# A projection stage with its triangular solution, gate columns and value columns in another order

## Chip, cores and metric

The kernel runs on one core of one Trainium2 chip. The metric is the device time in microseconds (us) of one execution; three executions of the kernel before are given. The engines are PE (TensorE, matmuls), PEld (its weight loads), DVE (VectorE), ACT (ScalarE), POOL (GpSimd) and SP (SyncE, which here only issues DMAs). Each runs its own list of instructions in order and waits on semaphores for the others.

## What is computed

A decoder trunk of two layers on x of 1024 tokens by 1024 features, float32. Only layer 0 is touched by the change:

```python
hn = rmsnorm(x, norm_w[0])
proj = hn @ w_in                                   # 1024 x IN0
gq, gk, gv, g_low, rw, gate = split(proj)          # q, k, values, low-rank gate input, RWKV part, gate
log_decay = log_sigmoid(g_low @ gk_up + gk_bias) / 16
o_a = gla_chunked(gq, gk, gv, log_decay)           # cumulated decay inside chunks of 64 tokens
...                                                # r, k, v, decay, a from rw with a token shift
o_b = rwkv7_scan(r, decay, k, v, -kk, kk * a)      # done in chunks of 64 tokens
o = concat(o_a, o_b) * silu(gate)
h = x + o @ w_out
```

The chunked form of the RWKV scan needs, for each chunk and head, the inverse of a unit triangular 64x64 matrix. In the kernel this is "the solution" (`solve`). There are 128 such matrices (16 chunks x 8 heads), one on each partition.

## The kernel before

All of layer 0's input projection is one stage, `project0`. It computes 30 weight tiles of 128 output features, called tile 0 to tile 29 by their turn. A tile is 48 matmuls of 128x512: eight k blocks, two halves of 512 tokens, and three products, since each float32 factor is split into a rounded high part and a low rest (`WH`, `WL` for the weights, `HNH`, `HNL` for the activations). `W0_ORDER` says which weights come in which turn:

- tile 0, and tiles 1 to 12: the shifted inputs and r, k, v for four pairs of heads. DVE and ACT work them up (`mix`, `keep_raw`).
- tiles 13 to 20: the gate. ACT applies SiLU (`keep_gate`) into `gate_row` and stores it to `gate_dram`.
- tile 21: the low-rank gate input (16 rows). Four small matmuls (L495) turn it into the decay's argument.
- tiles 22 to 25: q and k of the gated linear attention, kept in `QK` (`keep_qk`).
- tiles 26 to 29: its values, kept in `GV`.

What each engine does for a tile: SP loads its weights (`WA`, `WBK` or `WRAW`), POOL makes the high part (L1371) and the low part (L1375) once the tile two before is done (`split_parts`), PE waits for both parts and for `tile_kept` of the tile two before (its PSUM banks), ACT copies the result out of PSUM.

The solution runs on DVE. ACT stores the pairs' masked products to `bonds_dram` (`store_bonds`), loads them back with one matrix per partition into `X` (L569), and DVE does 62 steps of one multiplication and one addition (L666, L669). `X` lies in the four rows of `GV`, its product `TMP` in a row of `QK`. So tile 25 (the last row of `QK`) is kept only when the solution is over (`act.wait_ge(solved, ...)`). Then ACT stores `X` to `solved_dram`, waits for that, and only then uses `GV` for the decay of the linear attention: bias, absolute value, exponential, logarithm, a masked cumulated sum over 1024 tokens (L720), exponentials. DVE multiplies q and k with these (L728). Only then are tiles 26 to 29 kept in `GV`.

A block of code ends for all engines together (a barrier). The next one, `chunks0`, walks through the 1024 tokens in eight steps of two chunks. It loads the inverses (`TT0`, `TTB`) and the gate (`SG`) back from memory.

Of the kernel before, what the change touches and what calls it, by code (L numbers as in the profile page):

```python
# [22 lines left out]
F = mybir.dt.float32  # L23
# [7 lines left out]
P = 128  # L31
T = 1024
# [30 lines left out]
W0_GATE = 13  # L63
W0_GLOW = 21
W0_GLA = 22
W0_TILES = 30
W0_ORDER = list(range(13)) + list(range(22, 30)) + list(range(13, 22))
# [4 lines left out]
def trunk(nc, x, w0t, wup, gkup, wout0, w1t, wv1, bv1, wout1, par, bout1, fnorm, ident_d, istack_d, bdones_d,  # L72
          maska_d, scan_d, maskd_d, maskb_d, cos_d, sin_d, band_d, out):
    root = ExitStack()
    with root:
# [132 lines left out]
        with layer0:  # L208
# [3 lines left out]
            QK = VQ[:, PAIRS:, :].rearrange("p (a q) t -> p a q t", a=2)  # L212
# [3 lines left out]
            TT0 = [RAW[:, 1 - n // 2, n % 2 * HB:(n % 2 + 1) * HB].rearrange("p (q m) -> p q m", m=C) for n in range(4)]  # L216
            bonds_dram = nc.dram_tensor("bonds_dram", (TT, 2, PAIRS, 2, C, C), F, kind="Internal").ap()
            solved_dram = nc.dram_tensor("solved_dram", (TT, 2, PAIRS, 2, C, C), F, kind="Internal").ap()
            solved_out = sem("solved_out")
            G = sb("G", [P, PAIRS, NC], ctx=layer0)  # L220
# [4 lines left out]
            gate_out = sem("gate_out")  # L225
            half1 = ExitStack()
            with half1:
# [9 lines left out]
                WRAW = RAW[:, 0, 0:T].rearrange("p (k c) -> p k c", k=KT)  # L237
# [14 lines left out]
                with nc.Block() as block:  # L252
                    @block.sync
                    def _(sp):
# [7 lines left out]

                project0(nc, sem, PS, HNH, HNL, WA, WBK, WRAW, WH, WL, parts, wup_sb, xw, gkup, gate_row,
                         gate_dram, gate_out, RAW, scanm, scan_d, AR, BK, VT, QK, GV, bdones, G, GG, small, w0t, col, const2_in,
                         w_in, maska, TT0, bonds_dram, solved_dram, solved_out)
# [4 lines left out]
            with loop:  # L270
                chunks0(nc, sb, sem, loop, PS, AR, BK, VT, QK, GV, G, GG, small, ident, istack, maska, bdones, TT0,
                        solved_dram, solved_out, SG, col("gla_norm"), bk_tiles, wout0, wo_in, gate_dram, gate_out)
# [71 lines left out]

def project0(nc, sem, PS, HNH, HNL, WA, WBK, WRAW, WH, WL, parts, wup_sb, xw, gkup, gate_row, gate_dram,
             gate_out, RAW, scanm, scan_d, AR, BK, VT, QK, GV, bdones, G, GG, small, w0t, col, const_in, w_in, maska,
             TT0, bonds_dram, solved_dram, solved_out):

# [5 lines left out]
    mixd, kmix, kk, sa = (QK[:, i // 2, i % 2, :] for i in range(4))  # L354
    nrm, cum, e2, sw = (GV[:, i, :] for i in range(4))
    e1a, sq, scan_again = sw, nrm, gate_row
    gk_sb = kmix[0:16, 0:256]
    PAIRED = 3 * PAIRS + 1
    X = GV[:, :, :].rearrange("p a t -> p (a t)").rearrange("p (j i) -> p j i", i=C)
    ST, TMP = kmix, sa  # L360

    def arrival(n):
        return WA[:] if n % 2 == 0 or n == PAIRED else WBK if n < PAIRED else WRAW
# [32 lines left out]
    with nc.Block() as block:  # L396
        @block.sync
        def _(sp):
            sp.dma_start(scanm, scan_d).then_inc(scan_in, 16)
            for n in range(2, W0_TILES):  # L400
# [12 lines left out]
            sp.wait_ge(g_rel, GP)  # L413
# [4 lines left out]
            sp.wait_ge(tt0_in, 64)  # L418

        @block.gpsimd  # L420
        def _(pool):
            for n in range(2, W0_TILES):
                pool.wait_ge(w_in[n % 2], 16 * (n // 2) + 16)
                pool.wait_ge(tile_done, n - 1)
                split_parts(pool, arrival(n), WH[:, n % 2], WL[:, n % 2], 2 * n, parts)

        @block.tensor
        def _(pe):
# [57 lines left out]
            tile(W0_GATE, W0_GATE % 2)  # L486
            bonds(PAIRS - 1)
            for n in range(W0_GATE + 1, W0_GLA + 1):
                tile(n, n % 2)
# [3 lines left out]
            for j in range(GP):  # L493
                for h in range(2):
                    last = pe.matmul(PS[4 + 2 * j + h][:], gk_sb[:, j * P:(j + 1) * P], mixd[0:16, h * HB:(h + 1) * HB],  # L495
                                     start=True, stop=True)
                last.then_inc(gz_done, 1)

            for n in range(W0_GLA + 1, W0_TILES):
                tile(n, n % 2)  # L500
# [1432 lines left out]
```

## Time and profile before

| | |
|---|---|
| median of 3 executions | 1244.69 us (1243.75 to 1245.27) |
| the profiled execution's own time | 1252.05 us |
| its span | 1249.8 us |
| PE busy / PEld busy | 1124.4 us (90%) / 899.1 us (72%) |
| DVE / ACT / POOL busy | 662.6 / 332.7 / 294.0 us |
| mean granted TensorE clock | 0.95 of full speed |

All times inside the kernel below are microseconds from the start of the profiled span. `project0` fills the stretch from about 30 us to 446 us, `chunks0` follows until about 625 us. The profile gives PE's busy share in 40 slices of 31 us; it is 90% or more for nearly all of `project0`, but 6, 4 and 5 tenths in the slices that hold 344 to 437 us. Idle time before an instruction is put down to the instruction that released it.

### The profile page before, as it was taken

Reading aid. Unit: us, or ns where it says so; the run is one execution under the profiler, and the core shown is the slowest. Engines: PE = TensorE matmul, PEld = TensorE weight load, DVE = VectorE, ACT = ScalarE, POOL = GpSimd, SP = SyncE. Lnnn points to the kernel's source line nnn. Section 1 sums busy time; section 2 is a strip of 40 time slices with the busy share of each in tenths; the row PEclk is TensorE's granted clock in tenths of the full one; section 3 lists DMA queues with packets and bytes.
Section 4 is the critical chain, followed back from the end, with each engine's and each line's share of the span. In section 5 each row is a group of like instructions: output and inputs, shape, how many; then the busy total and the mean of one; then the engine's idle time right before and its main releaser. Section 6 shows DMA issues by size and latency. Waiting matters only on the chain. (4 is left out here: it accounts for less than half of the span.)

```text
span 1249.8 us, 20321 instructions
## 1 busy us (share of the span) xinstructions
PE 1124.4 (90%) x8408; PEld 899.1 (72%) x8408; DVE 662.6 (53%) x1031; ACT 332.7 (27%) x749; POOL 294.0 (24%) x190
## 2 busy tenths in 40 slices
PE   3999999999964578898889997999999899998997
PEld 3777777888753468787734446888888788887886
DVE  5288898499995315344434115255510258987233
ACT  6333423101103314233241003011110224554121
POOL 2222322334331011010000004133322534440500
PEclk9999999999987799999989998999999959999999
DMA  5211211632111060200204201111111010131011
GB/s 193 68 51 35 53 49 41 214 101 84 34 51 67 18 186 3 70 3 3 70 1 184 102 34 63 51 42 42 50 50 34 35 51 18 35 133 34 17 51 68
DMA packets 37577, 77.77 MB, mean 62 GB/s; under 512 B 19184, under 2 KB 19712, under 8 KB 37120
## 3 DMA queue, kind: packets, MB, share of 16 engines
q1 hardware_dynamic: 27616, 66.23, 15.9%
q10 hardware_dynamic: 9888, 10.49, 2.6%
q8 instruction: 56, 0.92, 0.3%
q14 instruction: 17, 0.14, 0.0%
HBM read 59.93 MB, written 16.78 MB: 61 GB/s over the span
## 5 line engine op out<-in xcount | busy, mean ns | idle before, releaser
L1383 PE MATMUL ps<-HNH,WH 128*128 128x512 f32 x896 | 356.2, 398 | 51.1 <-ACT GV L508 25.8
L1383 PE MATMUL ps<-HNH,WL 128*128 128x512 f32 x896 | 352.4, 393 | 0.0
L1383 PE MATMUL ps<-HNL,WH 128*128 128x512 f32 x896 | 352.0, 393 | 0.0
L1383 PEld LDWEIGHTS ps<-HNH,WH 128*128 128x128 f32 x896 | 170.4, 190 | 89.9 <-issue 54.4
L1383 PEld LDWEIGHTS ps<-HNH,WL 128*128 128x128 f32 x896 | 170.8, 191 | 36.3 <-issue 1.2
L1383 PEld LDWEIGHTS ps<-HNL,WH 128*128 128x128 f32 x896 | 170.6, 190 | 36.4
L1282 PE MATMUL ps<-BK,SG 128*128 128x512 f32 x256 | 112.8, 601 | 1.4 <-PEq L787 1.4
L1282 PEld LDWEIGHTS ps<-BK,SG 128*128 128x128 f32 x256 | 49.3, 193 | 63.7 <-issue 63.7
L1744 ACT ACTIVATE GV<-GV,nm 128x256 f32<-128x256 f32 x128 | 64.3, 504 | 78.6 <-DVE nm L1765 78.3
L666 DVE TENSOR_TENSOR VQ<-GV 128x62 f32<-128x62 f32 (+30 forms) x62 | 71.4, 1152 | 20.2 <-DMA GV<-bonds_dram 18.1
L1704 PE MATMUL ps<-V,GV 128*128 (+1 forms) x512 | 73.2, 292 | 0.8 <-DVE GV L1778 0.7
L1704 PEld LDWEIGHTS ps<-V,GV 128*128 128x128 f32 x512 | 70.9, 214 | 2.5 <-issue 1.3
L1765 DVE CUSTOM_DVE_ANT_0 GV<-ps,GV,nsink 128x256 f32<-128x256 f32 x128 | 56.8, 481 | 29.1 <-PE ps L1383 21.6
L669 DVE TENSOR_TENSOR GV<-GV,VQ 128x62 f32<-128x62 f32 (+30 forms) x62 | 68.9, 1111 | 2.1
L1371 POOL CAST WH<-WA 128x1024 fp32r<-128x1024 f32 x16 | 20.8, 1297 | 147.2 <-PE ps L1383 130.8
L508 ACT ACTIVATE RAW<-ps 128x512 f32<-128x512 f32 x42 | 22.9, 597 | 115.6 <-PE ps L1383 105.8
L1371 POOL CAST WH<-GV 128x1024 fp32r<-128x1024 f32 x18 | 18.7, 1041 | 145.3 <-PE ps L1383 138.8
L1693 PE MATMUL ps<-ident,GV 128*128 128x128 f32 x256 | 47.4, 314 | 0.5 <-ACT GV L1744 0.5
L1778 DVE COPY GV<-ps 128x512 f32<-128x512 f32 x64 | 44.0, 688 | 1.0 <-PE ps L1693 0.9
L1361 DVE TENSOR_TENSOR H<-ps,AR 128x512 f32<-128x512 f32 x16 | 10.3, 686 | 64.6 <-PE ps L1282 61.0
L1816 DVE TENSOR_SCALAR nsink<-par 128x16 f32<-128x16 f32 x1 | 1.0, 1039 | 81.1 <-PEq L1515 81.1
L1375 POOL TENSOR_TENSOR WL<-GV,WH 128x1024 fp32r<-128x1024 f32 x18 | 43.2, 2400 | 3.0 <-POOL WH L1371 2.9
(246 smaller groups left out, 1728.9 us busy)
## 6 DMA issues: line engine op xcount, KB each, us to landing
GV<-in_w1t SPq DMA_DIRECT2D x18, 512.0 KB, 3.6
AR<-in_x SPq DMA_DIRECT2D x16, 512.0 KB, 7.1
WA<-in_w0t SPq DMA_DIRECT2D x16, 512.0 KB, 3.6
RAW<-in_w0t SPq DMA_DIRECT2D x8, 512.0 KB, 3.7
gate_dram<-RAW ACTq DMA_DIRECT2D x8, 512.0 KB, 2.6
SG<-gate_dram SPq DMA_DIRECT2D x1, 4096.0 KB, 15.4
BK<-in_wout SPq DMA_DIRECT2D x4, 1024.0 KB, 6.8
h_dram<-H SPq DMA_DIRECT2D x8, 512.0 KB, 2.6
```

Source lines behind the costliest of these rows:

```text
L508: ins = act.activation(dst[:, h * HB:(h + 1) * HB], tile_bank[n % 2][h][:], func, **kw)
L666: dve.tensor_tensor(tmp, X[:, j:j + 1, j + 1:C].to_broadcast([P, j, n]), X[:, 0:j, j:j + 1].to_broadcast([P, j, n]), ALU.mult).then_inc(so ...
L669: dve.tensor_tensor(X[:, 0:j, j + 1:C], X[:, 0:j, j + 1:C], tmp, ALU.add).then_inc(solved, 1)
L1282: last = pe.matmul(PS[2 * (t % 4) + h][:], SG[:, k, t * P:(t + 1) * P], W[:, k, h * HB:(h + 1) * HB], start=(k == 0), stop=(k == KT - 1))
L1371: eng.tensor_copy(high, raw).then_inc(parts, 1)
L1375: eng.tensor_tensor(low, raw, high.bitcast(F), ALU.subtract).then_inc(parts, 1)
L1383: last = pe.matmul(out, a, b, start=(k == 0 and i == 0), stop=(k == n - 1 and i == 2))
L1693: last = pe.transpose(PS[4 + j % 2][:, (2 * a + b) * P:(2 * a + b + 1) * P], PR[:, j % 2, a, b * P:(b + 1) * P], ident[:])
L1704: last = pe.matmul(PS[6 + j // HT][:, (j % HT) * P + a * C:(j % HT) * P + (a + 1) * C], PT[:, j % 2, a, b * P:(b + 1) * P], V1[:, ds(n + b ...
L1744: ins = act.activation(PR[:, j % 2, a, :], SC[:, j % 2, a, :], ACT.Exp, scale=-1.0, bias=nm[:, h:h + 1], accum_out=rs[:, h:h + 1])
L1765: ins = dve.tensor_tensor_reduce(SC[:, j % 2, a, :], PS[2 * (j % 2) + a][:, 0:2 * P], band[:, 0 if first else 1, :], -1.0, nsink[:, h:h + ...
L1778: dve.tensor_copy(PT[:, j % 2].rearrange("p a k -> p (a k)"), PS[4 + j % 2][:]).then_inc(s["pt_kept"], 1)
```

## The change

Four parts lie in `project0`, the fifth in `chunks0`.

1. **Order of the tiles.** Tile 13 is now the low-rank gate input, tiles 14 and 15 the first two gate tiles, 16 to 19 the values, 20 to 23 q and k, 24 to 29 the other six gate tiles.
2. **Places.** `X` now lies in the upper half of `VQ` (`XS`), the product `TMP` in the first row of `RAW` (`solve_row`). Every gate, value, q and k tile is kept in the one `gate_row`; values go out to a new `value_dram`. The decay's rows and, after them, q and k lie in `GV`. The third arrival place for weights, `WRAW`, is gone: from tile 13 on every tile's weights arrive in `WA`.
3. **Work on the engines.** The decay's work on DVE stands inside the solution: `gate_sizes` before step 10, `gate_sums` before step 26. The cumulated sum is 16 scans of 64 tokens instead of one of 1024. From tile 16 on ACT makes the high part of the weights (`high_part(n + 2)`, ahead of keeping tile n). POOL makes the low part only, and multiplies q and k with their factors. SP stores the finished `X`.
4. **Waits.** The solution's end holds up no tile. The load of tile 14's weights now stands behind SP's wait for `pair_done` of the fourth pair. The block's end waits for the inverses of the first two steps, all gate stores and all value stores.
5. **`chunks0`.** The values are loaded back in two halves (`VG`), ahead of the gate. The zeroing of `S` and `GS` moves from DVE to POOL. PE waits for `consts` only ahead of the matmuls with `cen`.

```diff
-W0_ORDER = list(range(13)) + list(range(22, 30)) + list(range(13, 22))
+W0_ORDER = list(range(14)) + [22, 23] + list(range(18, 22)) + list(range(14, 18)) + list(range(24, 30))
...
     def arrival(n):
-        return WA[:] if n % 2 == 0 or n == PAIRED else WBK if n < PAIRED else WRAW
+        return WA[:] if n % 2 == 0 or n >= PAIRED else WBK
...
             for n in range(2, W0_TILES):
-                sp.wait_ge(parts, 2 * n if n in (PAIRED, PAIRED + 1) else 2 * n - 2)
-                if n == PAIRED + 2:
-                    sp.wait_ge(mixed, PAIRED)
-                if n == PAIRED + 5:
-                    sp.wait_ge(ab_out, 64 * PAIRS)
+                sp.wait_ge(parts, 2 * n if n >= PAIRED else 2 * n - 2)
+                if n == W0_GLOW + 1:
+                    sp.wait_ge(pair_done, PAIRS)
                     sp.dma_start(gk_sb, gkup).then_inc(gk_in, 16)
                 sp.dma_start(arrival(n), w0t[W0_ORDER[n]]).then_inc(w_in[n % 2], 16)
-            sp.wait_ge(gate_out, 16 * KT)
-            sp.dma_start(scan_again, scan_d).then_inc(gk_in, 16)
+            sp.wait_ge(solved, 2 * (C - 2))
+            sp.dma_start(solved_dram.rearrange("n e p h j i -> (n e p h) j i"), X).then_inc(solved_out, 16)
             sp.wait_ge(solved_out, 16)
-            sp.wait_ge(g_rel, GP)
             for n in range(2):
                 for e in range(2):
                     sp.dma_start(TT0[n][e * C:(e + 1) * C], solved_dram[n, e].rearrange("p h j m -> j (p h) m")
                                  ).then_inc(tt0_in, 16)
             sp.wait_ge(tt0_in, 64)
+            sp.wait_ge(gate_out, 16 * KT)
+            sp.wait_ge(value_out, 16 * 4)
...
                 pool.wait_ge(tile_done, n - 1)
-                split_parts(pool, arrival(n), WH[:, n % 2], WL[:, n % 2], 2 * n, parts)
+                if n < CAST:
+                    split_parts(pool, arrival(n), WH[:, n % 2], WL[:, n % 2], 2 * n, parts)
+                else:
+                    pool.wait_ge(parts, 2 * n + 1)
+                    pool.tensor_tensor(WL[:, n % 2], arrival(n), WH[:, n % 2].bitcast(F), ALU.subtract).then_inc(parts, 1)
+                if W0_QK <= n - 2 < W0_QK + 4:
+                    j = n - 2 - W0_QK
+                    pool.wait_ge(tile_kept, n - 1)
+                    pool.wait_ge(g_exp, GP)
+                    pool.tensor_tensor(GV[:, j, :], GV[:, j, :], gate_row, ALU.mult).then_inc(g_scaled, 1)
...
+            def high_part(n):
+                if n < W0_TILES:
+                    act.wait_ge(w_in[n % 2], 16 * (n // 2) + 16)
+                    act.wait_ge(tile_done, n - 1)
+                    act.activation(WH[:, n % 2], arrival(n), ACT.Copy).then_inc(parts, 1)
...
-            act.wait_ge(solved, 2 * (C - 2))
-            keep_qk(3)
-            act.dma_start(solved_dram.rearrange("n e p h j i -> (n e p h) j i"), X).then_inc(solved_out, 16)
-            act.wait_ge(solved_out, 16)
...
+            def gate_sums():
+                for j in range(GP):
+                    z, l = (nrm, cum)[j], (e2, sw)[j]
+                    dve.wait_ge(gz_step, GP + j + 1)
+                    link(dve.scalar_tensor_tensor(out=z, in0=z, scalar=0.0, in1=l, op0=ALU.min, op1=ALU.subtract))
+                    for c in range(NC):
+                        ins = dve.tensor_tensor_scan(l[:, c * C:(c + 1) * C], chunk_mask[:], z[:, c * C:(c + 1) * C], 0.0,
+                                                     ALU.mult, ALU.add)
+                    link(ins)
+                    relative(l, z, GG[:, j, :])
+                    dve.tensor_copy(mid, mid).then_inc(g_rel, 1)
...
                 for j in range(1, C - 1):
+                    if j == EARLY:
+                        gate_sizes()
+                    if j == LATE:
+                        gate_sums()
```

ACT's row in the program before, from the store of the last pair's products on (names: `GV` holds `X` and then the decay, `VQ` holds q and k, `RAW` the gate row):

```order
L521 DMA bonds_dram<-VQ 64x8x64 x4
L569 DMA GV<-bonds_dram 128x4096
...
L562 DMA gate_dram<-RAW 128x1024
L574 ACTIVATE VQ<-ps 16x512 x2
L578 ACTIVATE small<-small 128x1
L508 ACTIVATE VQ<-ps 128x512 x8
L589 DMA solved_dram<-GV 128x4096
L594 ACTIVATE GV<-ps,par 128x512 x4
```

ACT's row after, of the same place and of the first value tile behind it (`VQ` holds `X`, `WH` is a high part):

```order
L536 DMA bonds_dram<-VQ 64x8x64 x4
L616 DMA VQ<-bonds_dram 128x4096
L577 ACTIVATE WH<-WA 128x1024
L523 ACT_TABLE_LOAD
L523 ACTIVATE RAW<-ps 128x512 x2
L597 DMA gate_dram<-RAW 128x1024
L622 ACTIVATE GV<-ps,par 128x512 x4
...
L577 ACTIVATE WH<-WA 128x1024
L523 ACTIVATE RAW<-ps 128x512 x2
L603 DMA value_dram<-RAW 128x1024
```

The store of the solution has left ACT's row, the decay's first step stands ahead of the second gate tile, and a high part stands ahead of each kept tile.

DVE's row after, around step 26 of the solution (`RAW` is the product, `VQ` is `X`, `GV` the decay's rows; the scans are printed as L704). Before, steps 25 and 26 stood side by side:

```order
L726 TENSOR_TENSOR VQ<-VQ,RAW 128x25x38
L702 SCALAR_TENSOR_TENSOR GV<-GV 128x1024
L704 SCALAR_TENSOR_TENSOR GV<-chunk_mask,GV 128x64 x16
...
L708 COPY small<-small 128x16
L702 SCALAR_TENSOR_TENSOR GV<-GV 128x1024
L704 SCALAR_TENSOR_TENSOR GV<-chunk_mask,GV 128x64 x16
...
L708 COPY small<-small 128x16
L723 TENSOR_TENSOR RAW<-VQ 128x962
```

The decay's sums now delay the solution's second half.

SP's row after, at the end of `project0`:

```order
L413 DMA GV<-in_gkup 16x256
L414 DMA WA<-in_w0t 128x1024 x16
L417 DMA solved_dram<-VQ 128x4096
L421 DMA RAW<-solved_dram 64x8x64 x4
L403 UNCONDITIONAL_BRANCH
```

All 16 weight loads from tile 14 on stand behind the load of `gk_sb`, and the solution's store and reload come last.

## Rows read from the trace of the kernel before

**Rows 1.** Who PE waited for, 200 to 450 us: total, times, longest
```profile
PE ps L1383 <- ACT GV L508: 25.8, 1, 25.8
PE ps L1383 <- ACT VQ L508: 18.7, 1, 18.7
```

**Rows 2.** Timeline of ACT: start, duration, line, operation, idle before and its releaser
```profile
227.22 1.09 ACT L508 ACTIVATE RAW<-ps 128x512 f32<-128x512 f32 x2 [8.04 <-PE ps L1383]
...
380.66 0.60 ACT L508 ACTIVATE VQ<-ps 128x512 f32<-128x512 f32 x1 [38.15 <-DVE GV L669]
...
419.86 2.07 ACT L508 ACTIVATE GV<-ps 128x512 f32<-128x512 f32 x4 [4.77 <-DVE VQ L728]
433.77 1.09 ACT L508 ACTIVATE GV<-ps 128x512 f32<-128x512 f32 x2 [11.85 <-PE ps L1383]
444.65 1.09 ACT L508 ACTIVATE GV<-ps 128x512 f32<-128x512 f32 x2 [9.79 <-PE ps L1383]
```

**Rows 3.** Timeline of POOL: splits of tiles 14, 22 and 29
```profile
204.18 1.04 POOL L1371 CAST WH<-WA 128x1024 fp32r<-128x1024 f32 x1 [10.16 <-PE ps L1383]
205.31 2.39 POOL L1375 TENSOR_TENSOR WL<-WA,WH 128x1024 fp32r<-128x1024 f32 x1
...
305.55 3.22 POOL L1375 TENSOR_TENSOR WL<-RAW,WH 128x1024 fp32r<-128x1024 f32 x1
...
395.43 1.04 POOL L1371 CAST WH<-RAW 128x1024 fp32r<-128x1024 f32 x1 [28.22 <-PE ps L1383]
```

**Rows 4.** A stretch of PE: length, PE busy, granted clock, DMA share, GB/s
```profile
384.00:386.00 2.00, 2.00 (x6) 0.50 1.13 483
```

**Rows 5.** Timeline of DVE: solution's start, steps at 304 us, decay
```profile
236.12 0.18 DVE L666 TENSOR_TENSOR VQ<-GV 128x62 f32<-128x62 f32 x1 [18.07 <-DMA GV<-bonds_dram]
...
304.61 1.91 DVE L669 TENSOR_TENSOR GV<-GV,VQ 128x990 f32<-128x990 f32 x1
306.55 3.27 DVE L666 TENSOR_TENSOR VQ<-GV 128x992 f32<-128x992 f32 x1
309.85 1.19 DVE L669 TENSOR_TENSOR GV<-GV,VQ 128x992 f32<-128x992 f32 x1
...
408.55 2.29 DVE L720 TENSOR_TENSOR_SCAN GV<-RAW,GV 128x1024 f32<-128x1024 f32 x1
...
411.29 0.18 DVE L643 TENSOR_TENSOR GG<-GG,GV 128x15 f32<-128x15 f32 x1
411.51 1.23 DVE L644 TENSOR_TENSOR GV<-GV,small 128x1024 f32<-128x1024 f32 x1
```

**Rows 6.** Timelines of DVE and ACT around the last pair, 212 to 226 us
```profile
212.93 1.22 DVE L706 TENSOR_TENSOR BK<-VQ,GV 128x1024 f32<-128x1024 f32 x1
216.77 1.29 DVE L652 TENSOR_TENSOR VQ<-ps,maska 128x512 f32<-128x512 f32 x2
219.61 3.61 ACTq L521 DMA_DIRECT2D bonds_dram<-VQ  x4
225.24 0.34 ACTq L569 DMA_DIRECT2D GV<-bonds_dram  x1
```

**Rows 7.** DMAs by line (L408 weights, L589 solution out, L416 inverses in), and page part 6
```profile
DMA to landing us min/median/max: 3.5/3.6/7.2
...
DMA to landing us min/median/max: 6.3/6.3/6.3
...
DMA to landing us min/median/max: 3.0/3.2/3.8
...
gate_dram<-RAW ACTq DMA_DIRECT2D x8, 512.0 KB, 2.6
```

**Rows 8.** The same rounding cast on ACT in layer 1, from the critical chain
```profile
1149.93 1.07 ACT WH L1432
```

**Rows 9.** Timelines of SP and PE where `chunks0` starts
```profile
446.00 1.25 SPq L792 DMA_DIRECT2D RAW<-solved_dram  x2
...
448.04 1.07 PE L840 MATMUL ps<-ident,AR 128*128 128x128 f32 x4 [3.43 <-DVE cen L1226]
```

More of the change, by code:

```diff
@@ L270, in trunk @@
             with loop:
-                chunks0(nc, sb, sem, loop, PS, AR, BK, VT, QK, GV, G, GG, small, ident, istack, maska, bdones, TT0,
+                chunks0(nc, sb, sem, loop, PS, AR, BK, VT, QK, XS, value_dram, value_out, G, GG, small, ident, istack, maska, bdones, TT0,
                         solved_dram, solved_out, SG, col("gla_norm"), bk_tiles, wout0, wo_in, gate_dram, gate_out)
@@ L485, in _ @@
                     low_rank(p + 1)
-            tile(W0_GATE, W0_GATE % 2)
+            tile(W0_GLOW, W0_GLOW % 2)
             bonds(PAIRS - 1)
-            for n in range(W0_GATE + 1, W0_GLA + 1):
-                tile(n, n % 2)
+            tile(W0_GLOW + 1, (W0_GLOW + 1) % 2)
             pe.wait_ge(glow_kept, 1)
@@ new lines, in keep_gate, with keep_value @@
+            def keep_gate(n):
+                staged(n)
+                keep(n, gate_row, ACT.Silu)
+                act.wait_ge(tile_kept, n + 1)
+                act.dma_start(gate_dram[W0_GATES.index(n)], gate_row).then_inc(gate_out, 16)
+            def keep_value(n):
+                staged(n)
+                keep(n, gate_row, ACT.Copy)
+                act.wait_ge(tile_kept, n + 1)
+                act.dma_start(value_dram[n - W0_VALUE], gate_row).then_inc(value_out, 16)
+            act.wait_ge(pair_done, PAIRS)
@@ L608, in _ @@
                 act.activation(z, z, ACT.Exp, scale=1.0 / NORMALIZER).then_inc(g_exp, 1)
-            act.wait_ge(g_scaled, 4)
             for j in range(4):
-                keep(W0_GLA + 4 + j, GV[:, j, :], ACT.Copy)
+                staged(W0_QK + j)
+                keep(W0_QK + j, gate_row, ACT.Copy, scale=GLA_SCALE if j < 2 else 1.0)
+            for n in W0_GATES[2:]:
+                keep_gate(n)
         @block.vector
@@ L655, in keep_bonds, with gate_sizes @@
                 ins.then_inc(ab_kept, 1)
+            def gate_sizes():
+                for j in range(GP):
+                    z, l = (nrm, cum)[j], (e2, sw)[j]
+                    dve.wait_ge(gz_kept, j + 1)
+                    dve.scalar_tensor_tensor(out=l, in0=z, scalar=-1.0, in1=z, op0=ALU.mult, op1=ALU.max).then_inc(gz_abs, 1)
+            def gate_sums():
+                for j in range(GP):
+                    z, l = (nrm, cum)[j], (e2, sw)[j]
+                    dve.wait_ge(gz_step, GP + j + 1)
[6 more added lines that the diff above has]
+                    dve.tensor_copy(mid, mid).then_inc(g_rel, 1)
             def solve():
@@ L765, in chunks0 @@
     s = {n: sem("c_" + n) for n in names.split()}
-    tt_in = [sem(f"c_tt_in{n}") for n in range(NP)]
+    tt_in = {n: sem(f"c_tt_in{n}") for n in range(2, NP)}
+    vg_in = [sem(f"c_vg_in{h}") for h in range(2)]
     def after(eng, name, n):
@@ L795, in _ @@
             sp.wait_ge(solved_out, 16)
-            inverses(2)
+            sp.wait_ge(value_out, 16 * 4)
+            for h in range(2):
+                cols = slice(h * HB, (h + 1) * HB)
+                sp.dma_start(VG[:, :, cols], value_dram[:, :, cols].rearrange("k p t -> p k t")).then_inc(vg_in[h], 16)
+                inverses(2 + h)
             sp.wait_ge(gate_out, 16 * KT)
             sp.dma_start(SG[:], gate_dram.rearrange("k p t -> p k t")).then_inc(s["gate_in"], 16)
-            for n in range(3, NP):
+            for n in range(4, NP):
                 inverses(n)
@@ L841, in turns_av @@
                 last.then_inc(s["r1a"], 1)
+                if n == 0:
+                    pe.wait_ge(s["consts"], 1)
                 for p in range(PAIRS):
@@ L939, in step @@
                 after(pe, "s_kept", 2 * n + e)
+                if n == 0 and e == 0:
+                    pe.wait_ge(s["zeros"], 1)
                 if e == 0:
```

127 lines of the change are left out of this document (63 added, 64 removed).

## The prediction, made before the changed kernel ran

> **What bounds the kernel now.** I read PE's waits first, since PE is busy 90% of the span and every stage hangs on it. Two stalls inside `project0` stand out: 18.7 us before tile 27 and 25.8 us before tile 28 [rows 1]. ACT's timeline gives their cause [rows 2]: the keeping of tile 25 waits 38.15 us for the solution's last addition (L669) and comes at 380.66, and the keeping of tile 26 waits for L728 until 419.86. After each stall PE runs at half clock for a while: 0.50 granted, the 1.2 GHz level, at 384 to 386 us after 18.7 us of idleness [rows 4]. An undisturbed tile takes 444.65 − 433.77 = 10.88 us [rows 2]. Tile 27 took 395.43 − 381.8 = 13.6 [rows 2, 3], 2.7 too long. Tile 28 took 433.77 − (395.43 + 25.8) = 12.5, 1.7 too long. So the solution and the decay cost PE 18.7 + 25.8 + 2.7 + 1.7 = 48.9 us here. `chunks0` starts on SP at 446.00 and on PE at 448.04 [rows 9].
>
> After the change two chains run side by side, and the later one sets the block's end: the stream of tiles on PE, and the solution on DVE with its way through memory. I work out both.
>
> **The stream of tiles.** It ends at 444.65 now. Without the stalls it would end at 444.65 − 48.9 = 395.8. A new stall comes in at tile 14, because SP's load of its weights now stands behind `pair_done` of pair 4, which DVE gives at 212.93 + 1.22 = 214.15 [rows 6]. Two issues take about 0.4, landing takes 3.6 [rows 7] and the split 1.04 + 0.08 + 2.39 = 3.5 [rows 3]. That makes 221.7. Before, split 14 was over at 207.7 [rows 3] and tile 14 ended at 227.22 [rows 2], so it started at 216.3. PE is then idle for some 5.5 us. It then runs at half clock for a while: I charge 1.8, near the 1.7 of tile 28, where the bounds are 0 and 2.7. Behind it in SP's queue stand the loads of all later tiles, each one split behind. They have time: tile 14 itself now ends at about 234.5. The small matmuls L495 move from after tile 22 to after tile 14 at the same price. The stream ends at 395.8 + 5.5 + 1.8 = 403.1. Keeping tile 29 takes 1.1 and its store 0.4 + 2.6 [rows 2, 7]: the stream's part of the block is over at 407.2.
>
> High parts on ACT cost PE nothing: the cast takes 1.07 on ACT [rows 8] against 1.04 on POOL, and per tile ACT has 1.07 + 1.09 us of work in 10.88. If ACT sits in a wait when a tile ends, its cast comes late, and POOL's low part with it. The cover is 10.88 − 1.07 − 3.2 = 6.6 us per tile. The tightest place is tile 20: ACT must first have the decay's exponentials, which need `gate_sums`. By the chain below these end at about 302, the exponentials 3 us later, and tile 20 is done at about 305. That costs nothing as long as the sums are over by 308.
>
> **The solution.** ACT now issues the last pair's stores at 216.77 + 1.29 = 218.1 instead of 219.61, since no gate tile stands ahead of them. So X is loaded at 225.24 − 1.5 = 223.7 and the first step comes at 236.12 − 1.5 = 234.6 [rows 5, 6]. The steps took 380.6 − 236.1 = 144.5 us. What changes in them:
> - POOL's casts go. The step at 304.61 took 1.91 beside a cast and the next 3.27 beside a subtraction, against 1.19 undisturbed [rows 5]: 0.72 for a cast, 2.08 for a subtraction. Twelve splits fell into the solution, so −12 × 0.72 = −8.6.
> - The solution lasts longer and starts earlier, so it meets two more subtractions: +2 × 2.08 = +4.2.
> - Four multiplications of q and k on POOL, each a two-input operation like the subtraction: +4 × 2.08 = +8.3. Bounds: 0 if they fall beside nothing, 4 × 3.22 = 12.9 [rows 3] if each blocks DVE for its whole span.
> - `gate_sizes`: 2 × 1.23 = +2.5 [rows 5]. ACT adds the bias within some 8 us of tile 14's end, by 243; by the sizes of the first nine steps the tenth starts 11 us after 234.6. So no wait, with 3 us to spare.
> - `gate_sums`, twice: 1.23 + 1.23 for the two long operations, four short ones of about 0.2, and sixteen scans of 64. A scan of 1024 takes 2.29 and an operation of 15 elements 0.18 [rows 5], so one of 64 is 0.18 + 64/1024 × 2.1 = 0.31 by itself. Without a wait between them their fixed parts overlap partly: bounds 0.14 and 0.31, taken 0.21. That is 16 × 0.21 + 2.46 + 0.8 = 6.6, twice = +13.2. Bounds 10.9 and 16.5.
>
> The sum is 144.5 − 8.6 + 4.2 + 8.3 + 2.5 + 13.2 = 164.1, and the solution ends at 234.6 + 164.1 = 398.7. The store lands 6.3 later [rows 7]. Four loads follow, 0.65 apart and 3.2 to land [rows 7]: 5.2. With 0.3 for the barrier the next block starts at 398.7 + 6.3 + 5.2 + 0.3 = 410.5. That is 3 us behind the stream, so the solution still sets the end, now through memory and no longer through ACT's queue.
>
> The Trainium skill speaks against the short scans: VectorE: DVE Perf Modes, in the section on the TRN2 errata, says that SBUF operands cost a fixed time per instruction, many small tiles pay it each, and operands should have 512 elements or more. By its (N + 151)/0.96 ns rule for a float32 operation, the 30 extra scans cost 30 × 0.157 = 4.7 us, an estimate from that page; with it the sum would be some 2.7 us longer. The trace's nearest row is the 0.18 of 15 elements, which agrees in size and says nothing on overlap.
>
> **`chunks0`.** PE started 2.04 after the block because it waited for `cen` behind two memsets. Now the transposes start at once, at 410.6, and `cen` is ready under them. The loads of the values and the gate are needed only one step later, behind other work. PE will have been idle for 7 us, before it was 3.43 us [rows 9]. A colder start can cost up to tile 28's 1.7; I charge 0.5, since the clock may already have fallen in the shorter pause.
>
> **The sum.** PE's start in `chunks0` moves from 448.04 to 410.6 + 0.5 = 411.1: 36.9 us less. Later stages are the same instructions in the same order. Against the profiled execution that is 1252.05 − 36.9 = 1215.1. That execution is 7.4 above the median, so in the median 1244.69 − 36.9 = **1207.8 us**.
>
> **The rivals.**
> *The tiles end last.* If POOL's multiplications cost DVE nothing and the scans are cheap, the solution's end moves up by 10, but the stream's end at 407.2 + 0.3 stays: 3 us less, 1204.8. For it: the two chains are 3 us apart on 160. Against it: all twelve splits disturb DVE alike.
> *The solution is longer.* Whole-span blocking by POOL (+4.6), scans without overlap (+3.3) make 1215.7. The Trainium skill's SBUF — State Buffer, on who interferes with whom, has DVE and GpSimd hold a shared port exclusively for a whole instruction and the other block fully; an estimate by it is that +4.6. The trace shows 2.08 of 3.22 per subtraction, less than that rule read at its worst.
> *A stall inside the stream.* `gate_sums` wait for late logarithms or ACT's cast for late exponentials, at tiles 20 to 22. The first 3 us are covered by the solution. Beyond them each us counts: with 8 us of stall, 1212.8.
> *Slower than before: one arrival place.* From tile 13 on the load of tile n + 1 waits for the low part of tile n. The loop is landing + ACT's cast + POOL's subtraction, 3.6 + 1.1 + 3.2 = 7.9 of 10.88 us. It decides from a landing of 6.6 on; one load did take 7.2, beside X's load [rows 7]. With 10 us each the 14 tiles would take 3.4 × 14 = 48 longer and give back all: 1244.69 + 8 = 1253. Nothing moves much data during those tiles except stores of 512 KB, so I hold it unlikely.
> *The change doesn't do what it says.* Tile 27 could still wait for something of DVE's. Its keep now waits only for the gate's store, so this is part of the second last case.
>
> **How the numbers follow.** Forecast as worked out, 1206 to 1210: 0.45. Tiles end last: 0.20, 1203 to 1206. Longer solution: 0.18, 1210 to 1217. Stall inside the stream: 0.14, 1208 to 1216. One arrival place: 0.03. The range 1203 to 1215 leaves out about 0.2. A measurement of this kernel tells apart about 0.2% (2.5 us). All cases but the last lie far beyond it: faster 0.96, same 0.01, slower 0.03.
>
> **What would show it.** In the changed kernel's profile: no PE wait over 10 us in `project0`, one of about 5.5 before tile 14, and tiles 10.88 apart from tile 16 on. Steps of the solution beside POOL show one lengthened operation per tile, not two. The scans stand about 0.2 apart. The last L726 comes at about 399, and the first inverses land at about 410, after the last gate store. PE's first wait in the next block is for nothing of DVE's constants. It is wrong if the last store of a gate tile comes later than the inverses, or if PE waits for `parts` from tile 16 on.

## The result and the profile after

The changed kernel takes 1206.42 us (median of four executions; 1244.79 before), a ratio of 0.9668 with a 95% interval of 0.9615 to 0.9722. An execution that ran as a whole at a lower granted clock, here one of 1242.50 us, is left out of this and every later ratio, while the medians hold all. Forecast were 1207.8 us, 1203 to 1215. The profiled execution took 1206.31 us with a span of 1204.5.

PE's waits in `project0` and at the start of `chunks0` in the changed kernel (who waited for whom: total, times, longest). Against [rows 1] both long stalls are gone. The new one before tile 14 is there; the second row is the pause at the block's end:

```profile
PE ps L1435 <- POOL WL L1427: 5.9, 1, 5.9
PE ps L887 <- PEq L403: 4.3, 1, 4.3
```

ACT's timeline of the changed kernel: the last two gate tiles and the store of the last (start, duration, line, operation, idle before). The tiles stand 10.88 apart up to the end, against [rows 2]:

```profile
391.79 1.09 ACT L523 ACTIVATE RAW<-ps 128x512 f32<-128x512 f32 x2 [8.84 <-PE ps L1435]
...
402.67 1.09 ACT L523 ACTIVATE RAW<-ps 128x512 f32<-128x512 f32 x2 [9.79 <-PE ps L1435]
403.79 0.33 ACTq L597 DMA_DIRECT2D gate_dram<-RAW  x1
```

POOL's timeline of the changed kernel, the split of tile 14 (compare the first two of [rows 3]):

```profile
217.57 1.04 POOL L1423 CAST WH<-WA 128x1024 fp32r<-128x1024 f32 x1 [24.30 <-DMA WA<-in_w0t]
218.68 2.34 POOL L1427 TENSOR_TENSOR WL<-WA,WH 128x1024 fp32r<-128x1024 f32 x1
```

DVE's timeline of the changed kernel: the solution's first product, the second row of scans, two products beside POOL's subtraction and multiplication, and the last addition (compare [rows 5]):

```profile
230.09 0.18 DVE L723 TENSOR_TENSOR RAW<-VQ 128x62 f32<-128x62 f32 x1 [12.72 <-DMA VQ<-bonds_dram]
...
290.84 3.03 DVE L704 TENSOR_TENSOR_SCAN GV<-chunk_mask,GV 128x64 f32<-128x64 f32 x16
...
306.41 3.26 DVE L726 TENSOR_TENSOR VQ<-VQ,RAW 128x986 f32<-128x986 f32 x1
309.70 2.87 DVE L723 TENSOR_TENSOR RAW<-VQ 128x990 f32<-128x990 f32 x1
312.60 1.19 DVE L726 TENSOR_TENSOR VQ<-VQ,RAW 128x990 f32<-128x990 f32 x1
...
391.03 0.28 DVE L726 TENSOR_TENSOR VQ<-VQ,RAW 128x62 f32<-128x62 f32 x1
```

The timelines of SP and PE of the changed kernel at the end of the block (compare [rows 9]):

```profile
391.34 0.33 SPq L417 DMA_DIRECT2D solved_dram<-VQ  x1
397.81 2.71 SPq L421 DMA_DIRECT2D RAW<-solved_dram  x4
406.94 0.39 SPq L840 DMA_DIRECT2D VQ<-value_dram  x1
...
406.91 1.09 PE L887 MATMUL ps<-ident,AR 128*128 128x128 f32 x4 [4.34 <-PEq L403]
```

And what SP waited for last in `project0`:

```profile
SPq L425 <- DMA gate_dram<-RAW: 5.9, 1, 5.9
```

PE starts `chunks0` at 406.91 instead of 448.04, 41.1 us earlier. The last wait of the block is for the store of the last gate tile (L425), not for the inverses. Four inverse loads leave SP from 397.81 on over 2.71 us, and the gate store is issued at 403.79. Their times to landing (the loads of L421, then all gate stores of L597, of which the last took 2.6):

```profile
DMA to landing us min/median/max: 2.9/3.0/3.1
...
DMA to landing us min/median/max: 2.6/2.6/6.0
```

So the last inverse is there at about 402.9 and the gate store at 406.4. The solution, forecast to end the block, had 3.5 us of slack in this profile, and the stream of tiles ended it.

The spans differ by 45.3 us and the medians by 38.4. The stages behind `project0` explain this. The next views show them for the kernel before and for the changed one: `chunks0` with the output mix up to the load of x; from there to attention; attention up to the reload of h. The columns are the stretch, its length, PE's busy time with its instructions, the granted clock, and the share and GB/s of DMA.

Kernel before:

```profile
446.00:671.76 225.76, 192.10 (x3689) 0.96 0.15 46
671.76:991.13 319.37, 310.68 (x1305) 0.99 0.18 64
991.13:1113.12 121.99, 119.74 (x912) 0.83 0.12 35
```

Changed kernel:

```profile
406.90:635.53 228.63, 196.72 (x3689) 0.94 0.18 55
635.53:953.18 317.65, 308.89 (x1305) 0.99 0.19 64
953.18:1068.40 115.22, 113.29 (x909) 0.88 0.12 37
```

The block's start moves by 39.1 us. Then `chunks0` takes 2.9 longer at a granted clock of 0.94 instead of 0.96, the middle 1.7 less, and attention 6.8 less at 0.88 instead of 0.83. The code of the last two is the same. The profiled execution of before lay 7.4 us above its median, and its attention ran long at half clock; the last section returns to this. A fairer pair is the profile of before and the second one of the changed kernel (the first experiment), whose attention took 122.0 and 121.7 us: there the spans, 1249.8 and 1210.0, differ by 39.8.

### The profile page after: what moved, and what is told of

Same layout as the page of the kernel before. It is cut to its first block and busy times, and to the rows that moved or that the text cites. A ratio compares the mean times of both kernels' runs of the same rounds, so it can differ in the third digit from the quotient of the medians.

```text
span 1204.5 us, 20383 instructions
## 1 busy us (share of the span) xinstructions
PE 1117.0 (93%) x8408; PEld 893.1 (74%) x8408; DVE 652.9 (54%) x1055; ACT 344.0 (29%) x762; POOL 286.5 (24%) x182
## 5 line engine op out<-in xcount | busy, mean ns | idle before, releaser
L723 DVE TENSOR_TENSOR RAW<-VQ 128x62 f32<-128x62 f32 (+30 forms) x62 | 66.2, 1068 | 14.8 <-DMA VQ<-bonds_dram 12.7
L726 DVE TENSOR_TENSOR VQ<-VQ,RAW 128x62 f32<-128x62 f32 (+30 forms) x62 | 71.9, 1160 | 2.1
L1756 PE MATMUL ps<-V,GV 128*128 (+1 forms) x512 | 70.3, 284 | 0.8 <-DVE GV L1830 0.7
L1756 PEld LDWEIGHTS ps<-V,GV 128*128 128x128 f32 x512 | 67.7, 206 | 2.4 <-issue 1.2
L436 POOL TENSOR_TENSOR WL<-WA,WH 128x1024 fp32r<-128x1024 f32 x14 | 40.1, 2866 | 104.7 <-ACT WH L577 104.7
L1423 POOL CAST WH<-GV 128x1024 fp32r<-128x1024 f32 x18 | 18.7, 1041 | 143.6 <-PE ps L1435 137.3
L523 ACT ACTIVATE RAW<-ps 128x512 f32<-128x512 f32 x58 | 31.3, 592 | 67.2 <-PE ps L1435 67.2
L577 ACT ACTIVATE WH<-WA 128x1024 fp32r<-128x1024 f32 x14 | 14.9, 1062 | 120.4 <-PE ps L1435 120.4
L1413 DVE TENSOR_TENSOR H<-ps,AR 128x512 f32<-128x512 f32 x16 | 10.3, 686 | 64.6 <-PE ps L1334 60.9
```

Of the source, the lines that this page charges most:

```text
L436: pool.tensor_tensor(WL[:, n % 2], arrival(n), WH[:, n % 2].bitcast(F), ALU.subtract).then_inc(parts, 1)
L523: ins = act.activation(dst[:, h * HB:(h + 1) * HB], tile_bank[n % 2][h][:], func, **kw)
L723: dve.tensor_tensor(tmp, X[:, j:j + 1, j + 1:C].to_broadcast([P, j, n]), X[:, 0:j, j:j + 1].to_broadcast([P, j, n]), ALU.mult).then_inc(so ...
L726: dve.tensor_tensor(X[:, 0:j, j + 1:C], X[:, 0:j, j + 1:C], tmp, ALU.add).then_inc(solved, 1)
L1423: eng.tensor_copy(high, raw).then_inc(parts, 1)
L1756: last = pe.matmul(PS[6 + j // HT][:, (j % HT) * P + a * C:(j % HT) * P + (a + 1) * C], PT[:, j % 2, a, b * P:(b + 1) * P], V1[:, ds(n + b ...
```

## The experiments

In what follows, PE's start of `chunks0` is counted from the keeping of tile 12 (ACT's line L508 or L523, a few lines off in some edited kernels, at 201.7 to 204.1 us), since the program's first stages shift by some 2 us from one execution to the next. In the changed kernel's three profiles it is 203.6, 202.5 and 203.8. "View A" is that the stream of tiles with its last store ends the block, "view B" the prediction's, that the solution does.

### The changed kernel again

> The changed kernel once more, unaltered, as the measure for the runs beside it. Inside project0 and at the start of chunks0 its times should repeat those of its first profile to 0.3 us: last tile kept from 402.7, the solution's last addition over at 391.3, PE's first matmul of chunks0 at 406.9. What should differ from execution to execution is the length of the half-clock stretch at the start of layer 1's attention (27 us in the first profile, 40 us in that of the kernel before). If that stretch alone carries the spread of 1197 to 1206 us, then the difference of this run's span from 1204.5 is half the difference of the stretches.

Median 1208.29 us, ratio to before 0.9657 (0.9597 to 0.9718). The profiled execution took 1211.82. PE started `chunks0` at 404.17, 2.7 us earlier than first seen, more than the 0.3 expected: 1.6 of it lie ahead of tile 12's keeping and 1.1 in the stream. Behind the small matmuls that follow tile 14 (L510) the first profile has PE at half clock from 238.3 to 241.7 (0.51 granted), the second does not (1.00). The solution's store landed after 7.4 us and not 6.5, so the last inverse was there at 402.5, only 1.1 us ahead of the last gate store (403.7). Attention took 121.7 us against 115.2 in the first profile and the stage ahead of it 1.8 more; less the earlier start this makes about the 5.5 by which the span is longer. So most of the spread inside one kernel is the clock of the later stages. The expected half of the difference in half-clock time would be 6.8 for attention (41.0 against 27.3 us); it was 6.5.

### Tile 14's weights first

```diff
-                if n == W0_GLOW + 1:
-                    sp.wait_ge(pair_done, PAIRS)
-                    sp.dma_start(gk_sb, gkup).then_inc(gk_in, 16)
                 sp.dma_start(arrival(n), w0t[W0_ORDER[n]]).then_inc(w_in[n % 2], 16)
+                if n == W0_GLOW + 1:
+                    sp.wait_ge(pair_done, PAIRS)
+                    sp.dma_start(gk_sb, gkup).then_inc(gk_in, 16)
```

> Tile 14's weights are loaded ahead of the wait for the fourth pair, only the small load for the decay stays behind it. Both views: the 5.9 us stall before tile 14 and about 2 us of half clock behind it go, the last tile is kept from 394.7 instead of 402.7. View A (in the changed kernel the stream of tiles with its last gate store ends the block, the inverses are there 3.5 us earlier): PE starts chunks0 3.6 us earlier, at 403.3, set now by the inverses. View B (the prediction's: the solution ends the block): PE starts at 406.9 as before, gain 0.

The stall is gone and the last tile is kept from 395.33. From the keeping of tile 12 that is 193.3 us instead of 199.3: 6.0 us and not 8, since part of the half clock behind the stall came back elsewhere. SP's waits at the block's end:

```profile
SPq L417 <- DVE VQ L726: 21.7, 1, 21.7
SPq L421 <- DMA solved_dram<-VQ: 6.0, 1, 6.0
SPq L425 <- DMA gate_dram<-RAW: 1.7, 1, 1.7
SPq L403 <- DMA RAW<-solved_dram: 1.3, 1, 1.3
```

PE's start comes 200.1 from tile 12's keeping, 3.4 us earlier than in the changed kernel's first profile and 2.3 earlier than in its second. View A gave 3.6, view B 0. Now the inverses end the block by 1.3 us, and only about half of what the stream gained is seen. Median 1197.51 us, 0.9602 (0.9541 to 0.9663). That is 10.8 under the changed kernel's 1208.29, three times what the start gained; in the profiled execution attention took only 105.5 us, so the medians do not measure this edit.

### High parts on POOL again

```diff
-    CAST = W0_GLOW + 3
+    CAST = W0_TILES
...
     (high_part issues nothing)
```

> The high parts of tiles 16 to 29 are made by POOL again, as in the kernel before; all else as in the changed kernel. Each of the 13 splits that fall into the solution should lengthen it by 0.72 us, 9.4 in all: last addition over at 400.7, inverses at 412.3. Tiles stay 10.88 apart. View A: PE starts chunks0 at 412.6, 5.7 us later (9.4 less the 3.5 of slack). View B: 9.4 us later. A third view, that ACT's casts do not matter because DVE isn't slowed by a cast: no change.

DVE's timeline beside one split shows both lengthened operations again, and the third is the one beside a multiplication:

```profile
306.12 1.89 DVE L726 TENSOR_TENSOR VQ<-VQ,RAW 128x972 f32<-128x972 f32 x1
308.04 3.25 DVE L723 TENSOR_TENSOR RAW<-VQ 128x980 f32<-128x980 f32 x1
311.32 2.86 DVE L726 TENSOR_TENSOR VQ<-VQ,RAW 128x980 f32<-128x980 f32 x1
```

The solution takes 171.5 us (230.2 to 401.7) against 161.2: 10.3 longer, expected 9.4. The expectation counted 13 casts inside the solution and there are 14: 14 × 0.72 = 10.1. PE starts `chunks0` at 413.59, 210.1 from tile 12's keeping, 6.6 later. View A gave 5.7, or 6.8 with the 10.3, and view B 9.4, or 10.3. PE's waits in the stream are unchanged. So ACT's casts shorten the solution, and 3.7 us of that were not needed. Median 1215.69 us, 0.9729 (0.9666 to 0.9792).

### The solution made longer

```diff
+                    if 50 <= j < 57:
+                        dve.wait_ge(solved, 2 * (j - 1))
+                        link(dve.tensor_tensor(TMP, TMP, XS[:, 0, :], ALU.mult))
```

> Seven additional multiplications of 1024 elements stand in the solution (steps 50 to 56), 7 x 1.26 = 8.8 us of DVE, and nothing else changes. View A (3.5 us of slack): PE starts chunks0 5.3 us later, at 412.2. View B (no slack): 8.8 us later, at 415.7.

The solution takes 8.9 us more. PE's first matmul of `chunks0`:

```profile
412.55 1.09 PE L890 MATMUL ps<-ident,AR 128*128 128x128 f32 x4 [10.76 <-PEq L403]
```

That is 208.8 from tile 12's keeping, 5.2 later than in the first profile, 6.3 later than in the second. View A gave 5.3 and view B 8.8. The slack was thus 3.7 us measured from the first profile and 2.6 from the second, whose stream was 1.1 us faster. Median 1217.85 us, 0.9724 (0.9665 to 0.9783).

### No wait for stores at the block's end

```diff
             sp.wait_ge(tt0_in, 64)
-            sp.wait_ge(gate_out, 16 * KT)
-            sp.wait_ge(value_out, 16 * 4)
...
                 sp.dma_start(VG[:, :, cols], ...).then_inc(vg_in[h], 16)
-                inverses(2 + h)
             sp.wait_ge(gate_out, 16 * KT)
+            for h in range(2):
+                inverses(2 + h)
```

> The end of project0 no longer waits for the gate and value stores; chunks0 waits for the gate stores before it writes the second pair of inverses over the gate row. If the last gate store ends the block in the changed kernel (view A), PE starts chunks0 once tile 29 is kept, 1.4 us after its last matmul instead of 4.2 us: 2.8 us earlier, at 200.8 us from the keeping of tile 12 instead of 203.6. If the inverses end it (view B), nothing moves. The second pair of inverses comes about 2 us later and costs nothing.

PE starts at 405.19, 201.3 from tile 12's keeping. That is 2.3 us earlier than in the changed kernel's first profile, but the edit's share is less: the stream was as fast here as in the second profile (no half clock behind the small matmuls), and against that the start is 1.2 earlier. PE's pause at the block's end says the same: 3.22 us against 4.34 and 4.37. So the stores did end the block, as in view A, but only 1.1 of view A's 2.8 came. The solution's store took 7.4 us to land here and not 6.5 (399.61 is the first inverse's issue), so the inverses ended the block, right behind. Its times (1195 to 1225, median 1217.4) say nothing of the edit: in the profiled execution attention alone took 133.9 us, at a granted clock of 0.75.

### The decay's sums at step 34

```diff
-    EARLY, LATE = 10, 26
+    EARLY, LATE = 10, 34
```

> The decay's sums stand before step 34 of the solution instead of step 26, all else as in the changed kernel. Eight steps of 2.4 us and one or two of POOL's subtractions come ahead of them, 22 us, so the sums end at 319 and ACT's exponentials at 323 instead of 302. ACT then casts tile 22's high part from 323 and POOL's low part is done at 327, while PE wants tile 22 at 315.6. Expected: one PE wait of 11 us before tile 22 with 2 us of half clock behind it, last tile kept 13 us later, PE's start of chunks0 13 us later. The prediction's rival of a stall inside the stream has this price per us; its cover of 3 us at tile 20 means that step 26 to 28 costs nothing. If the cover is larger than thought, the wait is shorter by as much.

PE's waits:

```profile
PE ps L1435 <- POOL WL L436: 11.2, 1, 11.2
PE ps L1435 <- POOL WL L1427: 5.8, 1, 5.8
```

One wait of 11.2 us for tile 22's low part, as expected. PE starts `chunks0` at 420.30, 216.6 from tile 12's keeping: 13.0 later, and 13 was expected. The rival of a stall inside the stream has its price right, and it did not happen because the sums came in time. Median 1212.52 us, though its attention ran nearly all at full clock (105.5 us).

### One wait put back

```diff
             def keep_gate(n):
                 staged(n)
+                if n == 25:
+                    act.wait_ge(solved, 2 * (C - 2))
```

> The changed kernel with one wait put back: ACT keeps tile 25 only when the solution is over, as in the kernel before (there the fourth tile of q and k, here a gate tile, whose storage has nothing to do with the solution). Expected: tile 26 is done at about 370, tile 27 waits for the keeping of tile 25 until about 392.5, so one PE wait of 22 us with 2 to 3 us of half clock behind it; last tile kept 25 us later and PE's start of chunks0 25 us later than in the changed kernel, at 228.5 from the keeping of tile 12. If the gain came from elsewhere than this wait and the decay behind it, the start moves by clearly less.

```profile
PE ps L1437 <- ACT RAW L523: 18.4, 1, 18.4
PE ps L1437 <- POOL WL L1429: 5.8, 1, 5.8
```

The stall is 18.4 us, where the kernel before had 18.7 [rows 1]. PE starts `chunks0` at 427.99, 224.3 from tile 12's keeping, 20.8 us later. Expected were 22 and 25. The solution ended at 387.6 here, 3.7 earlier than in the changed kernel, since a stopped stream makes no weight parts on POOL either: 12 subtractions fell into it and not 14, at 2.08 us each. Median 1227.07 us, 0.9847 (0.9805 to 0.989), against 1207.54 for the changed kernel on the same chip: 19.5 us. So this one wait, with no other part undone, costs half of the gain. The other half is put down to the decay's work, which stood behind the solution and made the second stall of 25.8 us [rows 1], and which stays inside it here; no run puts that back.

### `chunks0` with the constants of before

```diff
-            pool.memset(S[:], 0.0).then_inc(s["zeros"], 1)
-            pool.memset(GS[:], 0.0).then_inc(s["zeros"], 1)
...
+            dve.memset(S[:], 0.0).then_inc(s["zeros"], 1)
+            dve.memset(GS[:], 0.0).then_inc(s["zeros"], 1)
...
+            pe.wait_ge(s["consts"], 1)
             turns_av(0)
```

> In chunks0 S and GS are zeroed by DVE ahead of cen and PE waits for it at the start, as in the kernel before; project0 as in the changed kernel. Expected: PE's first matmul of chunks0 comes 2.0 us after the block's start instead of 0, and the first matmul with the inverses (line of solve) 11.0 instead of 9.3 us after it. If PE's start was bound by the clock or by ACT anyway, the second number stays within 0.5 of 9.3.

PE's first matmuls and the first with an inverse:

```profile
408.75 1.12 PE L885 MATMUL ps<-ident,AR 128*128 128x128 f32 x4 [6.33 <-DVE cen L1276]
...
416.95 1.96 PE L937 MATMUL ps<-AX,RAW 64*64 64x128 f32 x32 [0.70 <-ACT AX L1114]
```

PE's first matmul is 2.0 late, but the first with an inverse comes 10.2 us after the block's start, where 11.0 was expected and the changed kernel's first profile has 9.3: 0.9 of the 2.0 reaches it. The stretch from the block's start to the load of x took 225.7 us against 228.0 to 228.8 in the changed kernel. That looked as if the edit cost more than it gains; the last experiment tests it. Median of two executions 1210.46 us, 0.971 (0.9653 to 0.9767).

### Both ends overlapped

```diff
                 (tile 14's weights first, as above)
...
-            sp.wait_ge(solved_out, 16)
-            for n in range(2):
-                for e in range(2):
-                    sp.dma_start(TT0[n][e * C:(e + 1) * C], ...).then_inc(tt0_in, 16)
-            sp.wait_ge(tt0_in, 64)
-            sp.wait_ge(gate_out, 16 * KT)
-            sp.wait_ge(value_out, 16 * 4)
...
             sp.wait_ge(solved_out, 16)
+            inverses(0)
+            inverses(1)
             sp.wait_ge(value_out, 16 * 4)
...           (inverses of steps 2 and 3 behind gate_out, as above)
-                if n >= 2:
-                    pe.wait_ge(tt_in[n], 32)
+                pe.wait_ge(tt_in[n], 32 if n >= 2 else 64)
```

> Three edits on the changed kernel: tile 14's weights first (as in e1), no wait for stores at the block's end (as in e4), and the solution's way through memory reaches into chunks0: its store is waited for there and PE waits for the first inverses ahead of the first use, 9.3 us into the block. Expected: last tile kept from 395, PE starts chunks0 at 396.7, 10.2 us earlier than in the changed kernel and 5.5 earlier than in e1; inverses of steps 0 and 1 land at 403, before their use at 406, so no new wait. Median of all 10 us under the changed kernel's. Rival: PE then waits at the first use for the inverses (5 us or more), since their loads compete with those of values and gate; then the gain is about 5.

> The changed kernel again, for a comparison with the two below on the same chip. PE's start of chunks0 202.4 to 203.6 us after the keeping of tile 12; from the block's start to the load of x behind chunks0 228.0 to 228.6 us, as in its first two profiles.

> The overlap version again, beside the changed kernel: PE's start of chunks0 at 192.3 from the keeping of tile 12, 10 to 11 us ahead of the changed kernel's; median of the undisturbed runs 7 to 11 us lower. If chunks0 eats the gain (it took 229.7 us in this version's first profile, 1 to 2 more than in the changed kernel), the difference is nearer to 7.

The changed kernel's third profile has 203.8 and 228.8 us, each 0.2 above what was expected. In the overlap version's first profile PE starts `chunks0` at 395.44, 192.1 from tile 12's keeping: 11.5 us ahead of the changed kernel's first, where 10.2 were expected. At the first use of the inverses it then waits a little:

```profile
PE ps L936 <- DMA RAW<-solved_dram: 1.4, 1, 1.4
```

The median was 1199.70 us, 0.9618 (0.9573 to 0.9664). In the second profile it starts 195.2 from that point, 2.9 later than expected, and does not wait there for the inverses at all. The stream alone was 3.2 us longer, with 6.8 us at half clock from 227.3 on that the first profile does not have. Beside the changed kernel on one chip the medians are 1196.25 and 1207.54 us, with ratios to before of 0.9598 (0.9568 to 0.9629) and 0.9696 (0.9665 to 0.9726): 11 us less. Its start gained 8.5 in this profile and 11.5 in the other. The ratio of the version with tile 14's weights first alone, 0.9602, cannot be told from either, since attention's chance lengths lie on all of them. Spans of profiles with the same attention can be compared. With 115.3 us of it, the overlap version's 1194.4 stands 10.1 and 10.7 below the changed kernel's 1204.5 and 1205.1. With 105.5 us, its 1182.7 stands 7.2 below the 1189.9 of tile 14's weights alone. So this is the fastest version by its profiles; the medians do not show it.

### The same with the constants of before

> The overlap version with the constants of chunks0 as in the kernel before. With the constants put back, the stretch from chunks0's start to the load of x took 225.7 us against 228.0 to 228.6 with the changed constants. View C (the constants' edit starts PE 1.9 us earlier but costs the block more than that, through a colder clock in its first steps): the stretch is 2 to 3 us shorter than in the overlap version and the whole kernel 1 to 3 us faster. View D (the 225.7 was chance, PE's clock in that stretch varies by this much): the stretch is as long or up to 2 us longer than in the overlap version, and the kernel is no faster.

Median 1198.93 us, 0.9632 (0.9599 to 0.9665), against 1196.25 with the changed constants. The stretch from the block's start to the load of x took 229.8 us, as long as in the overlap version's first profile (230.0), while that version's second took 224.3. View D holds: one and the same kernel shows 230.0 and 224.3, with 27 and 17 us at half clock. The 225.7 above also had 17, against 24 to 30 in the changed kernel. So it was the clock's chance, and no loss by the edit is shown. Nor is a gain; the 2 us of an earlier start are below what the spread lets one see.

## Why the prediction came out, and what was off

**The stalls' price.** 48.9 us for the two stalls and the half clock behind them were right: with them taken off and the new stall put on, the last tile was to be kept from 403.1; it was 402.67. Putting back the one wait gives a stall of 18.4.

**The new stall.** Forecast 5.5 us, found 5.9 (5.7 to 5.9 in all profiles that have it). Tile 14 ran from 221.07 to ACT's cast at 234.01, 2.1 over the undisturbed 10.88, and 1.8 was charged.

**The solution: the step that failed.** It was to end at 398.7 and ended at 391.3, so it did not end the block. By the prediction's own sign (wrong if the last gate store comes later than the inverses) this step failed. It began 4.5 us too late in the sum and was taken 2.9 too long (164.1 against 161.2):
- its start, 230.1 instead of 234.6. X's load was taken with the 10.7 us of before; it took 7.8. The stores ahead of it were issued in 2.66 us instead of 3.61 [rows 6], and the early stages were 0.7 us faster;
- POOL's multiplications: 2.87 against 1.19 beside each, 1.7 and not 2.08, 1.6 us in all;
- the sums: 6.3 each and not 6.6, without the subtraction that fell into each. Sixteen scans took 3.03 us, 0.19 each, against 2.29 for the one long scan;
- the sizes and the casts that went: 0.3 each.

The number of POOL's subtractions inside was right: 14, of which 12 lengthened a step by 2.1 and two a sum. Why X's load was shorter stays open. In the nine profiles where the code is the same up to it, it took 7.6 to 8.0 us in eight and 10.0 in one (the decay's sums at step 34); in the versions with tile 14's weights first it took 8.9 to 10.3. The solution's store took 6.3 to 7.4 in most profiles, 8.4 and 9.2 in one each. With 10.0 and 8.4 together, as that one profile has them, the inverses would have come some 4 us later in the changed kernel and ended the block; this is an estimate from these times. So the stream ended the block in the changed kernel's three profiles, by 3.5, 1.1 and 3.5 us, but that distance is no more than these two transfers vary by.

The stream's end stood 3 us behind in the working, and the rival of that name was given 0.20. Its cause there was cheap multiplications and scans; the real cause was mostly the earlier start. The time of that rival, 1204.8, and the forecast's 1207.8 both lie within 3 us of the median, so the time alone does not tell them apart. The experiments with a longer solution and a shorter stream do: of 8.9 and 10.3 us added to the solution 2.6 to 3.7 were not seen, and of the stream's 6.0 only 3.4.

The Trainium skill's VectorE: DVE Perf Modes, in the section on the TRN2 errata, put the fixed cost of the 30 extra scans at 4.7 us, an estimate from that page. The trace has 2 × (3.03 − 2.29) = 1.5. It agrees with the rule for a two-input operation by itself (1.23 us for 1024 elements), but in a row of scans without waits between them 0.19 us passed for each of 64 elements, so the fixed cost was not paid in full each time. The Trainium skill's SBUF — State Buffer, on who interferes with whom, has two-input operations of DVE contend with GpSimd's reads while ACT waits on no one. The undone casts agree: 0.72 us of DVE per cast on POOL, none on ACT. That the other engine blocks for the whole span is not borne out: DVE lost 2.1 us beside a subtraction of 2.3 to 3.4.

**`chunks0` and after.** The start gained 1.9 by the constants as said (4.34 us of idleness before PE and none after the barrier), but the stage as a whole took 2.9 longer, and 0.5 was charged. The longer part is half clock: the stretch had 0.94 granted against 0.96. The assumption that later stages take the same time is right for their instructions and wrong for their time: attention took 6.8 us less here, and over all profiles it ranges over 28 us.

**The sum.** 36.9 us were forecast for PE's start and 41.1 came. Of the 4.2 more, 2.9 went in `chunks0`, and the medians show 38.4. So the total was closer than its parts, and that is luck: the solution's end was 7.4 us too late in the sum but the stream stopped the gain after half of it, `chunks0` gave some back by a term that was left out, and attention's clock, which moves the time by more than the error of 1.4 us, was in no term.

**The rivals.** A stall inside the stream: did not occur, and its price is confirmed (11.2 us of wait, 13.0 at the end). One arrival place for the weights: no PE wait for `parts` from tile 16 on in the changed kernel, tiles 10.88 apart. A longer solution: no. Late wait of tile 27: none.

## To carry to other kernels

When two chains run into one barrier, work out both ends and the distance between them; a gain on the later one is worth that distance at most, and then the other must move too (here tile 14's load and the waits for stores). A wait at a barrier for data that the next block needs only microseconds later belongs at its use: moving three such waits together with tile 14's load brought PE's start 7 to 12 us forward, of which the load alone had given 2 to 4, by which profiles one compares. Before a saving of a few microseconds is believed or disbelieved, look whether another stage's clock moved by as much.

## What the runs showed of the hardware

Attention runs at half clock at its start for a time that is chance, though PE is busy there. One stretch of the kernel before and one of the changed kernel (length, PE busy, granted clock):

```profile
1018.00:1022.00 4.00, 4.00 (x21) 0.50 0.17 22
```

```profile
976.00:980.00 4.00, 4.00 (x23) 0.50 0.00 0
```

PE is busy for all of the 4 us in both, at the 1.2 GHz level. Three more profiles of the same stage, with unchanged code (the overlap version's second, the longer solution, and the one without the waits for stores):

```profile
940.71:1046.18 105.47, 103.16 (x910) 0.98 0.13 41
```

```profile
959.99:1081.93 121.94, 119.62 (x909) 0.83 0.11 35
```

```profile
952.89:1086.76 133.87, 131.85 (x912) 0.75 0.10 32
```

Over the fourteen profiles the stage took 105.5 (three), 115.2 to 115.4 (six), 121.7 to 122.0 (four) or 133.9 us (one), with 3, 27, 41 and 68 us at half clock, and nothing between. Each further us at half clock lengthened it by 0.41 to 0.44 us (9.7 for 23.9, 16.4 for 37.6, 28.4 for 64.9). The same program fell into different ones: the changed kernel into 115.2, 121.7 and 115.3. That is most of the difference between 1206.31 and 1211.82 us in two profiled executions of one kernel, and it can be why the profiled execution of before was 7.4 us above its median. The stage ahead (x's load to attention) tells one group apart: it took 317.6 to 317.7 us in exactly the six profiles with 27 us, and 319.1 to 319.5 in the other eight, which have a further 3.4 us at half clock in it. So the length is not drawn only when attention begins. What decides it, PE being busy before and after, stays open; no run was made for it.
